# Two-block network kernel: preparation of the grouped-query attention's queries and keys in the last layer, in narrow columns, at a changed side pace

## The reference

```python
def _rms_norm(x, g):
    xf = x.astype(jnp.float32)
    return (xf * lax.rsqrt(jnp.mean(xf * xf, axis=-1, keepdims=True) + RMS_EPS) * g).astype(x.dtype)

def _apply_axial_rope(x, cos, sin):
    x1, x2, x3, x4 = jnp.split(x, 4, axis=-1)
    rotated = jnp.concatenate([-x2, x1, -x4, x3], axis=-1)
    return (x * cos[:, None] + rotated * sin[:, None]).astype(x.dtype)
...
    gk_l = _apply_axial_rope(gk_l, cos, sin)      # keys, each normed over its head of 64
    gq_l = _apply_axial_rope(gqa_q(aq_l), cos, sin)
```

## Time and profile before

| | |
|---|---|
| Median of 3 runs | 4297.05 us (4296.63 to 4306.17) |
| The profiled execution, its device time | 4299.14 us |
| Its span, first to last instruction | 4297.2 us |
| PE busy | 4013.4 us, 93% |
| DVE busy | 2315.3 us, 54% |
| ACT busy | 1540.4 us, 36% |
| POOL busy | 757.1 us, 18% |
| Granted TensorE clock, mean | 0.976 |

### The profile page before, as it was taken

How to read it: one execution, slowest core, us unless ns; L and a number is a source line. 1 busy time by engine, 2 the same in 40 slices (tenths; PEclk the granted TensorE clock), 3 DMA queues, 4 the chain that set the end, 5 groups by cost and what they waited for, 6 DMA issues and landing times. The chain is left out here.

```text
span 4297.2 us, 87039 instructions
## 1 busy us (share of the span) xinstructions
PE 4013.4 (93%) x37024; PEld 2400.4 (56%) x37024; DVE 2315.3 (54%) x4059; ACT 1540.4 (36%) x2530; POOL 757.1 (18%) x920
## 2 busy tenths in 40 slices
PE   9998999899999999999989989899899978998998
PEld 4444975444444444555558866664454437885663
DVE  5762546787443233577534335567578643344556
ACT  3121355200000011233235556663234225655663
POOL 0001411000110000000023332240000014432240
PEclk9999999999999999999989999999999989999999
DMA  4333012344241554443442221232344442212231
GB/s 132 105 107 108 2 68 82 120 145 147 102 172 49 196 184 136 134 163 133 162 145 72 70 76 38 77 89 86 121 155 152 173 140 76 77 51 69 72 107 63
DMA packets 350384, 468.06 MB, mean 109 GB/s; under 512 B 56199, under 2 KB 253607, under 8 KB 349040
## 3 DMA queue, kind: packets, MB, share of 16 engines
q1 hardware_dynamic: 298176, 266.26, 20.3%
q0 software_dynamic: 51824, 196.24, 13.0%
HBM read 328.14 MB, written 147.86 MB: 111 GB/s over the span
## 5 line engine op out<-in xcount | busy, mean ns | idle before, releaser
L491 PE MATMUL psum<-arena 128*128 128x512 f32 x2352 | 1033.0, 595 | 17.3 <-issue 7.0
L491 PEld LDWEIGHTS psum<-arena 128*128 128x128 f32 x2352 | 446.2, 190 | 564.9 <-issue 546.3
L3357 PE MATMUL psum<-arena 64*64 64x64 f32 (+7 forms) x16704 | 538.3, 242 | 60.7 <-issue 31.6
L1079 PE MATMUL psum<-arena 128*128 128x512 f32 x1344 | 582.3, 594 | 9.4 <-DMA arena<-w_down 3.9
L706 PE MATMUL psum<-arena 128*128 128x512 f32 x1232 | 535.6, 594 | 6.2 <-DVE arena L772 2.7
L3357 PEld LDWEIGHTS psum<-arena 64*64 64x64 f32 (+2 forms) x16704 | 463.0, 141 | 130.2 <-issue 67.5
L1079 PEld LDWEIGHTS psum<-arena 128*128 128x128 f32 x1344 | 254.1, 190 | 327.8 <-issue 318.6
L2704 DVE CUSTOM_DVE_ANT_0 arena<-psum,arena 128x512 f32<-128x512 f32 (+3 forms) x532 | 293.5, 591 | 206.2 <-PE psum L2591 201.5
L706 PEld LDWEIGHTS psum<-arena 128*128 128x128 f32 x1232 | 232.0, 190 | 303.2 <-issue 291.2
L2653 ACT COPY arena<-psum 128x1024 f32<-128x1024 f32 (+3 forms) x290 | 244.9, 844 | 191.4 <-PE psum L2577 185.3
L2591 PE MATMUL psum<-arena 64*128 64x512 f32 (+3 forms) x1192 | 268.3, 543 | 19.2 <-DVE arena L2704 8.5
(11 more groups left out here) (367 smaller groups left out, 4807.4 us busy)
## 6 DMA issues: line engine op xcount, KB each, us to landing
arena<-w_in SPq DMA_DIRECT2D x86, 512.0 KB, 5.8
proj<-arena SPq DMA_DIRECT2D x172, 256.0 KB, 2.0
arena<-w_mod POOLq DMA_DIRECT2D x24, 1024.0 KB, 5.6
arena<-down_sum SPq DMA_DIRECT2D x40, 512.0 KB, 3.7
arena<-proj POOLq DMA_DIRECT2D x31, 640.0 KB, 5.1
arena<-proj SPq DMA_DIRECT2D x28, 640.0 KB, 7.6
arena<-w_down SPq DMA_DIRECT2D x30, 512.0 KB, 3.7
x_home<-arena POOLq DMA_DIRECT2D x26, 512.0 KB, 5.0
```

Of the source, the lines that this page charges most:

```text
L491: ins = pe.matmul(ps[:, b, :], L[:, k, :], R[:, k, :], start=(p in ("P1", "P5", "P6", "P7") and k == 0), stop=(k == KT // 2 - 1), skip_gro ...
L1079: ins = pe.matmul(self.bank(j, b), self.left(p, j, left, *g)[:, k - g[0], :], R[:, k - k0, :], start=(x in ("P1", "P5", "P6", "P7") and k ...
L3357: return pe.matmul(out, lhsT, rhs, start=first, stop=last, skip_group_check=not (first and last))
```

## The change

In the last layer only, `GqaPrep` gives way to a new class `GqaPrepNarrow`. It computes the same values in another arrangement:

- total(j) is ten products, each with 128 tokens' squares as the stationary side and two columns of `block_ones` as the moving side, into 20 columns of a PSUM bank of its own (the side lane's bank 3): token by (tile, head).
- ACT takes the root of those 20 columns ("std"), DVE their reciprocal ("inv").
- POOL copies the 20 columns into 1280, each repeated 64 times ("wide"), and PE transposes that in ten 128x128 pieces into PSUM ("turn"), where it stands feature by token.
- norm reads the factors from PSUM. rot, out, the stores and the loads are as before.
- There are 24 side steps. For tile j: turn(j) at g = 4 + 5j, total(j + 1) at 5 + 5j, rot(j) at 6 + 5j on PE; norm(j) at 5 + 5j, inv(j + 1) at 6 + 5j, out(j) at 7 + 5j on DVE; square(j + 1) at 4 + 5j, std(j + 1) at 6 + 5j on ACT; wide(j + 1) at 7 + 5j, the store of x(j) and the load of x(j + 2) both at 8 + 5j on POOL. Ahead of them stand square(0) at 0, total(0) at 1, std(0) and inv(0) at 2, wide(0) at 3.
- turn(j) waits for out(j - 1), since rot(j - 1) stands in the same banks.

The pace in the last layer has a second side step at each odd n from 93 on. So g = 0 to 4 stand at n = 88 to 92, then g = 5 and 6 at n = 93, 7 at 94, 8 and 9 at 95, 10 at 96, 11 and 12 at 97, 13 at 98, 14 and 15 at 99, 16 at 100, 17 and 18 at 101, 19 at 102, 20 and 21 at 103, 22 at 104, 23 at 105, and `leave` at n = 107.

```diff
--- before.py
+++ after.py
@@ -4023,6 +4023,201 @@
             yield
 
 
+class GqaPrepNarrow(Stage):
+
+
+
+    NT = TOK2 // P
+
+    def __init__(self, core, gemm, proj, kx, vx, cos, sin, par, at):
+        super().__init__(core)
+        self.gemm, self.proj, self.kx, self.vx, self.par = gemm, proj, kx, vx, par
...
+        self.wide, self.std, self.inv = R(at, TOK2), R(at + TOK2, 2, 2 * self.NT), R(at + TOK2 + 4 * self.NT, 2, 2 * self.NT)
...
+        self.s_pe = Steps(core.pe, "sum turn rot", 4)
+        self.s_act = Steps(core.act, "sq std", 4)
+        self.s_dve = Steps(core.dve, "inv norm out", 4)
+        self.s_pool = Steps(core.pool, "wide", 4)
+        self.steps = 24
+
+    def run_pool(self, pool):
+        c, E, Dv = self.c, self.s_pe, self.s_dve
+
+        def load(j):
+            self.gemm.wait_stored(pool, 13 + j)
+            pool.dma_start(self.x[:, j % 2, :], self.proj[(13 + j) * P:(14 + j) * P, :]).then_inc(c.moved[8 + j % 2].sem, 16)
+
+        def spread(j):
+            pool.wait_ge(Dv.sem, Dv.at(j, "inv"))
+            if j:
+                pool.wait_ge(E.sem, E.at(j - 1, "turn"))
+            wide = self.wide.rearrange("p (t d) -> p t d", d=64)
+            pool.tensor_copy(wide, self.inv[:, j % 2, :].unsqueeze(2).broadcast_to([P, 2 * self.NT, 64])).then_inc(self.s_pool.sem, 1)
+
+        load(0)
+        load(1)
...
+        yield
+        yield
+        yield
+        spread(0)
+        yield
+        for j in range(4):
+            yield
+            yield
+            yield
+            if j < 3:
+                spread(j + 1)
+            yield
+            pool.wait_ge(Dv.sem, Dv.at(j, "out"))
+            x, done = self.x[:, j % 2, :], c.moved[j % 2].sem
+            if j < 3:
+                pool.dma_start(self.proj[(13 + j) * P:(14 + j) * P, :], x).then_inc(done, 16)
+            else:
+                for g in range(2):
+                    for r in range(3):
+                        pool.dma_start(self.kx[(3 * g + r) * 64:(3 * g + r + 1) * 64, :],
+                                       x[64 * g:64 * g + 64, :]).then_inc(done, 16)
+            if j < 2:
+                pool.wait_ge(done, self.out[j] + 16)
+                load(j + 2)
+            yield
...
+    def run_pe(self, pe):
+        ps, E, A, Dv, O = self.c.psum, self.s_pe, self.s_act, self.s_dve, self.s_pool
+
+        def total(j):
+            pe.wait_ge(A.sem, A.at(j, "sq"))
+            if j:
+                pe.wait_ge(A.sem, A.at(j - 1, "std"))
+            for t in range(self.NT):
+                ins = pe.matmul(ps[:, 3, 2 * t:2 * t + 2], self.sq[:, j % 2, t * P:(t + 1) * P], self.c.const("block_ones")[:, 0:P:64],
+                                start=True, stop=True)
+            ins.then_inc(E.sem, 1)
+
+        def turn(j):
+            pe.wait_ge(O.sem, O.at(j, "wide"))
+            if j:
+                pe.wait_ge(Dv.sem, Dv.at(j - 1, "out"))
+            for t in range(self.NT):
+                ins = pe.transpose(ps[:, t // 4, t % 4 * P:t % 4 * P + P], self.wide[:, t * P:(t + 1) * P], self.c.const("ident"))
+            ins.then_inc(E.sem, 1)
+
+        yield
+        total(0)
+        yield
+        yield
+        yield
+        for j in range(4):
+            turn(j)
+            yield
+            if j < 3:
+                total(j + 1)
+            yield
+            pe.wait_ge(Dv.sem, Dv.at(j, "norm"))
+            for s in range(2):
+                ins = pe.matmul(ps[:, s, :], self.c.const("rope"), self.x[:, j % 2, CTX + 512 * s:CTX + 512 * s + 512],
+                                start=True, stop=True)
+            ins.then_inc(E.sem, 1)
+            yield
+            yield
+            yield
+
+    def run_act(self, act):
+        E, A, Dv = self.s_pe, self.s_act, self.s_dve
+
+        def square(j):
+            act.wait_ge(self.c.moved[8 + j % 2].sem, self.base[j % 2] + 16 * (j // 2 + 1))
+            if j > 1:
+                act.wait_ge(E.sem, E.at(j - 2, "sum"))
+            act.activation(self.sq[:, j % 2, :], self.x[:, j % 2, :], ACT.Square).then_inc(A.sem, 1)
+
+        def std(j):
+            act.wait_ge(E.sem, E.at(j, "sum"))
+            if j > 1:
+                act.wait_ge(Dv.sem, Dv.at(j - 2, "inv"))
+            scale = 1.0 if j < 3 else 1.0 / 64
+            act.activation(self.std[:, j % 2, :], self.c.psum[:, 3, 0:2 * self.NT], ACT.Sqrt, scale=scale,
+                           bias=EPS * 64 * scale).then_inc(A.sem, 1)
+
+        square(0)
+        yield
+        yield
+        std(0)
+        yield
+        yield
+        for j in range(4):
+            if j < 3:
+                square(j + 1)
+            yield
+            yield
+            if j < 3:
+                std(j + 1)
+            yield
+            yield
+            yield
+
+    def run_dve(self, dve):
+        ps, E, A, Dv, O = self.c.psum, self.s_pe, self.s_act, self.s_dve, self.s_pool
+
+        def inverse(j):
+            dve.wait_ge(A.sem, A.at(j, "std"))
+            if j > 1:
+                dve.wait_ge(O.sem, O.at(j - 2, "wide"))
+            dve.reciprocal(self.inv[:, j % 2, :], self.std[:, j % 2, :]).then_inc(Dv.sem, 1)
+
+        yield
+        dve.wait_ge(self.c.moved[10].sem, self.tab + 32)
+        yield
+        inverse(0)
+        yield
+        yield
+        for j in range(4):
+            x = self.x[:, j % 2, :]
+            yield
+            dve.wait_ge(E.sem, E.at(j, "turn"))
+            dve.scalar_tensor_tensor(out=x, in0=x, scalar=self.par("q_norm" if j < 3 else "k_norm", 0),
+                                     in1=ps[:, 0:3, :].rearrange("p a b -> p (a b)")[:, 0:TOK2],
+                                     op0=ALU.mult, op1=ALU.mult).then_inc(Dv.sem, 1)
+            yield
+            if j < 3:
+                inverse(j + 1)
+            yield
+            dve.wait_ge(E.sem, E.at(j, "rot"))
+            lat = x[:, CTX:TOK2]
+            dve.tensor_tensor(self.rot, ps[:, 0:2, :].rearrange("p a b -> p (a b)"), self.sin, ALU.mult)
+            dve.drain()
+            dve.tensor_tensor(lat, lat, self.cos, ALU.mult)
+            dve.drain()
+            dve.tensor_tensor(lat, lat, self.rot, ALU.add)
+            dve.drain().then_inc(Dv.sem, 1)
+            yield
+            yield
+
+
 GRID, WIN_R, WIN_C = 64, 8, 16
 NA_ROWS = 10
 NA_KEYS = NA_ROWS * GRID
@@ -4108,8 +4303,8 @@
         prep = RwkvPrep(side, gemm, proj, par, core.W[:, 4096:4096 + 4 * 384], a["lowrank"][l], rw, fac,
                         [(x_at, x_at + KT * TOK2), (room.areas[0][0], top), (4096 + 4 * 384, 8192)])
         na_band.gap, prep.gap = 8, 6
-        gemm.beside = [na_band, prep, GqaPrep(side, gemm, proj, kx, vx, a["rope_cos"], a["rope_sin"], par, x_at)]
-        gemm.pace = lambda n: n < 16 or n >= 20
+        gemm.beside = [na_band, prep, (GqaPrepNarrow if last else GqaPrep)(side, gemm, proj, kx, vx, a["rope_cos"], a["rope_sin"], par, x_at)]
+        gemm.pace = lambda n, last=last: (n < 16 or n >= 20) + (last and n >= 92 and n % 2)
         rwkv = Rwkv(core, rw, fac, y_dir, [(top - 64 - 10 * 384, top - 64), (h_at, h_at + KT * TOK2), (big, top - 64 - 10 * 384)],
                     (side.stage_end.sem, prep.meet), skip=CTX // P if last else 0)
         gemm.next_loads = rwkv.first_loads
```

More of the change, by code:

```diff
@@ L4023, in run_dve @@
             yield
+class GqaPrepNarrow(Stage):
[3 more added lines that the diff above has]
+        self.gemm, self.proj, self.kx, self.vx, self.par = gemm, proj, kx, vx, par
+        R = core.region
+        self.cos, self.sin = R(at, SEQ), R(at + SEQ, SEQ)
+        self.cos_src, self.sin_src = cos, sin
+        at += 2 * SEQ
+        self.x, self.sq, self.rot = R(at, 2, TOK2), R(at + 2 * TOK2, 2, TOK2), R(at + 4 * TOK2, SEQ)
+        at += 4 * TOK2 + SEQ
+        self.wide, self.std, self.inv = R(at, TOK2), R(at + TOK2, 2, 2 * self.NT), R(at + TOK2 + 4 * self.NT, 2, 2 * self.NT)
+        self.base = [core.moved[8 + i].planned for i in range(2)]
+        self.out = [core.moved[i].planned for i in range(2)]
+        for j in range(4):
+            core.moved[8 + j % 2].planned += 16
+            core.moved[j % 2].planned += 16 if j < 3 else 96
+        self.v_out = core.moved[2].planned
+        core.moved[2].planned += 96
+        self.tab = core.moved[10].planned
+        core.moved[10].planned += 32
+        self.s_pe = Steps(core.pe, "sum turn rot", 4)
[16 more added lines that the diff above has]
+        load(1)
+        pool.dma_start(self.cos, self.cos_src).then_inc(c.moved[10].sem, 16)
+        pool.dma_start(self.sin, self.sin_src).then_inc(c.moved[10].sem, 16)
+        self.gemm.wait_stored(pool, 17)
+        for g in range(2):
+            for r in range(3):
+                pool.dma_start(self.vx[(3 * g + r) * 64:(3 * g + r + 1) * 64, :],
+                               self.proj[17 * P + 64 * g:17 * P + 64 * g + 64, :]).then_inc(c.moved[2].sem, 16)
+        yield
[15 more added lines that the diff above has]
+            else:
+                for g in range(2):
```

(11 more changed lines are left out.)

## The result

The changed kernel takes 4335.56 us (4334.17 to 4342.71), the kernel before 4298.69 us beside it: a ratio of 1.008, 95% interval 1.0065 to 1.0094. It is slower, by 34 us by the ratio and 37 by the medians. The way was forecast; the size, 20.6 us, was not, and the range ended at 4328.

The account below looks back on a forecast made before the run. PE was taken to bound the kernel, busy 93% of the span. Work +6.6, waits +16.0 and clock -2.0 made +20.6 us on a median of 4297.05, about 4318 us; range 4306 to 4328.

Parts of the forecast that it names:

- The bound: PE, busy 93% of the span, bounds the kernel; the change touches PairProj's last 26 main steps in the last layer.
- The work: On PE, 1.48 us of transposes and 0.16 us for the narrow total per tile, +6.6 us for four tiles.
- The waits: PE's waits in the last layer's stretch, from turn(0) to `leave`, 33.1 us against 17.1 before, so +16.0 us.
- the contention at `leave`: Unit 12's last stores and Rwkv's first loads fall amid the `kx` stores, adding 3 us to a 10.6 us wait.
- The round trip: Store of x(j) to square(j + 2), 7.9 to 10.2 us from out(j): total(2) waits 4.2 us, total(3) 9.8.
- The clock: PE's slow time after long waits in the stretch, 6.7 us against 8.7 before, so -2.0 us.
- my signs of being wrong: In PE's timeline: total(2) or total(3) waiting under 3 us, `leave` under 6, or the stretch under 137 us.
- Rival D: Transposes of turn(0) and turn(1) lower PE's clock, two more slow stretches of 1.9 us: +24 us, 4322; chance 0.10.
- A: One round trip of x is covered, with a short first trip: about +10 us, 4307; chance 0.16.
- C: Rwkv's first loads go ahead of the last `kx` stores, both trips long: +31 us, 4328; chance 0.12.
- B: Faster: PE's waits inside the stage hang on DVE's reciprocals and nothing takes their place: -8.3 us, 4289; chance 0.06.

Follow-up runs that it names:

- e4: Changed kernel with PE's and DVE's semaphore counts numbered in program order; ratio 1.0070 to the kernel before, S 145.0 us.
- e3: Changed kernel with buffers of their own for x(2) and x(3), all loads at the start; ratio 1.0030 to the kernel before, S 130.0 us.
- e2: Changed kernel with 128 moving columns in the totals' products in place of 2; ratio 1.0046 to the kernel before, S 137.7 us.
- e8: e7's edits, but second side steps only at n = 99 and 108, gap of 20 in GqaPrep too; 4280.53 us, 0.9945 of the kernel before.
- e7: Changed kernel with own x buffers, 128-column totals, counts in program order and a gap of 20 together; ratio 0.9983 to the kernel before.
- e1: Changed kernel with the old pace, one side step at each main step; ratio 0.9999 to the kernel before, M 121.1 us.
- e6: Kernel before with the gap behind GqaPrep's last step raised from 2 to 20 side steps, both layers; ratio 0.9966 to the kernel before.
- e9: e8 with 2 moving columns in the totals again; ratio 0.9957 to the kernel before, S 101.9 us.
- e10: Changed kernel with the gap behind its side stage raised from 2 to 20; ratio 1.0050 to the kernel before, S 134.2 us.

## Why the prediction was right in its way and wrong in its size

- **The bound.** Right: the loss lies on PE in this stretch, 33.3 of the 34 to 37 us.
- **The work.** Forecast +6.6, measured +4.5. The transposes take 1.12 us for ten where four of them had given 0.148 each, and the narrow total takes no more than the wide one (2.15). The instructions on DVE, ACT and POOL were sized rightly: 0.28 us for the reciprocal, 1.55 for norm, 1.3 for the copy, as its row had said. The estimate of 1.9 us from the Trainium skill's GPSIMD Engine Reference, section 3.1, would have been 0.6 us too long here.
- **The waits.** Forecast 33.1, measured 33.8, each in its place. That the sums agree is luck, since errors cancel: turn(1) 0.9, turn(2) 1.6 and total(3) 1.2 over the forecast, `leave` 2.9 under it. I read the waits of POOL and ACT by their names and not by their counts; that step failed, and it costs 1.2 us at turn(1), 1.8 at turn(2), and some tenths at total(3) (e4). And the contention at `leave` was overrated: from the issue of the first `kx` store to PE's release it took 14.9 us (3527.91 to 3542.82), 1.3 more than before (3505.13 to 3518.71), where I had added 3. The rest of the 2.9 is mostly PE's slow clock behind rot(3): its three products took 11.6 us where I had 10.3, and it waited that much less.
- **The round trip.** Right as the cause, and the largest single wait (e3: 15.3 us with both). The size at total(2), 4.2 against 4.3, is luck. I had taken the short form there, 3.5 us from the store to the load; it took 5.4 (3453.65 to 3459.05), and the copy's 1.26 us stood ahead of the store, so that from the end of out(0) to the square it was 10.5 us and not 7.9. PE came later by as much: the same copy held turn(1), and turn(1) and the product behind it ran 1.5 us slow. The second trip took 12.6 us where I had 10.2, by the copy and by a load that needed 5.7 us (3487.59 to 3493.30) in place of 4.1.
- **The clock.** This is the term that failed. I took the mean excess after a wait, 1.9 us, twice and 2.9 once, and came to 6.7 us; it is 20.9. By place, against the forecast: from total(2) on 4.8 (1.9), from total(3) on 5.0 (1.9), behind `leave` 3.0 (2.9), behind rot(3)'s wait 2.2 (0), behind total(0) and from rot(0) on, with no idle time, 3.5 (0), and 1.5 from turn(1) on, which I had let vanish in the wait that follows; the rest are modelled tails. So the mean was too small for a total that runs slow itself and keeps the product behind it slow, and I priced nothing where PE had not just stood idle. The ten 2-column products of a total are no relief for a slow clock and can bring about one: e2, which changes nothing but their columns, brings the term to 9.6 and the ratio down by 0.0034. Of the forecast's error of 12.7 us in S (150.6 - 137.9) this term is 14.2, the work -2.2 and the waits 0.7. None of my signs of being wrong could catch it, since each was for a loss smaller than forecast.
- **Rival D** had a cause of this kind in the transposes. In e8 40 of them run in S, none behind a wait of over 1.6 us, and the mean granted clock of M is 1.00; turn(0), behind 1.5 us, is followed by a product at full clock in every profile. Whether the ten of turn(1) prolong the slow stretch behind their wait isn't separated: in e7 the product behind them takes 5.1 us in place of 3.4, after a wait of 3.4, and a wait of 3.7 without transposes had such a stretch too. The Trainium skill's TensorE: Matmul & The Clock Gate, Part 4, says of a transpose that it doesn't count as busy in the same way; the short groups of e8 show no loss by it.
- **Rivals A and C.** A's condition, a short first trip, didn't come about. C's did by half: both trips were long, but `leave` waited 2.9 us less than forecast where C had 4 more. Its 4328 lay nearest to the measured time for another reason than its own. **B** fell where it was said to: the trip and the four additions took the reciprocals' place.
- **What the pace does** was seen only in its pieces. The prediction never costed the narrow form at the old pace. e1 shows that it would have come out even, and that the loss is the pace's: 20.9 us of M in the wide form, 33.3 in the narrow one.

## What to carry to other kernels

Before steps of a side stage are moved closer together, count what must fit between two of them: a store and reload through DRAM took 8.6 (e1) to 12.6 us (the changed kernel), from the end of out(j) to the square, against 3.45 for a main step, and no engine's busy time shows it. A wait is worth what its count says, not its name; where names are numbered by tile but issued across tiles, a wait reaches further than it reads. And where a stage's last wait holds an engine for stores that nothing in the stage needs, moving the wait costs one line (e6: 0.9966).

## What the runs showed of the hardware

- Behind products with 2 moving columns TensorE's granted clock fell although the engine had not stood idle. In the windows shown, the mean granted clock behind such a total is 0.66 and 0.70 with two columns and 1.00 with 128, at 2.15 and 2.24 us for the 20 instructions. Of the totals with no wait, or one under 0.3 us, ahead of them, 10 of 16 are followed by a slow group in the six narrow kernels with 2 columns (changed, e1, e3, e4, e9, e10; e3's total(3), right behind a turn that had waited, is left out), at different tiles in different executions; in e2, e7 and e8, with 128 columns, none of 9 is. That 2-column products in an attention, are followed by usual rows is not contradicted: it doesn't happen each time. How it comes about stays open.
- Loading 128 columns of weights sets the time of such a product: the weight loads fill 2.14 of the 2.20 us of total(0)'s window, and 64 times as many moving columns cost 4% (2.15 and 2.24 us).
- The six `kx` stores, 2 MB together, each from 64 partitions, took 13.6 us from the first one's issue to PE's release in the kernel before, and 14.9 in the changed one, where Rwkv's first loads are issued in their midst.
